# A decoder step on Trainium2: group norm, new rows, block compression and tables in one stage, with gates, down weights and route order moved

## The reference, cut to what matters

```python
mod = silu(c) @ w_ada + b_ada
h = rmsnorm(x) * (1 + sc1) + sh1
proj = h @ w_in
o_nsa, cmp_new, slc_new, win_state = nsa_group(proj, ...)
o_rwkv, wkv_T = rwkv_group(h, ...)
x = x + gt1 * (concat([o_nsa, o_rwkv]) @ w_out)
h2 = rmsnorm(x) * (1 + sc2) + sh2
eid, ew = hier_route(h2, ...)
x = x + gt2 * moe_ffn(h2, eid, ew, ...)
```

```python
y = (y - mean(y)) * rsqrt(var(y) + GN_EPS) * ln_x_w + ln_x_b
return (y + bonus) * g, S_T
```

## Time and profile before

| | |
|---|---|
| runs | 2575.92, 2577.76, 2578.44 us; median 2577.76 |
| the profiled execution | 2578.24 us, of which the trace spans 2576.1 |
| TensorE busy | 2268.1 us (88% of the span) |
| VectorE, ScalarE, GpSimd busy | 714.6, 358.2, 73.2 us |
| read from and written to HBM | 686.11 MB, 19.86 MB |

### The profile page before, as it was taken

How to read it: one execution, slowest core, us unless ns; L and a number is a source line. 1 busy time by engine, 2 the same in 40 slices (tenths; PEclk the granted TensorE clock), 3 DMA queues, 4 the chain that set the end, 5 groups by cost and what they waited for, 6 DMA issues and landing times. The chain is left out here.

```text
span 2576.1 us, 47327 instructions
## 1 busy us (share of the span) xinstructions
PE 2268.1 (88%) x20283; PEld 1619.4 (63%) x20283; DVE 714.6 (28%) x1979; ACT 358.2 (14%) x823; POOL 73.2 (3%) x122
## 2 busy tenths in 40 slices
PE   6899999799999968787766996999999999899997
PEld 4567667677777757664544774566656566566654
DVE  1111211340132145535655115111122111112224
ACT  1000110211210000013422003010011100000003
POOL 0000000000000000001011001000000000000000
PEclk9999999899999967776878997999999999999999
DMA  9887787533344430007669307999999999999993
GB/s 319 340 317 302 294 332 291 146 104 112 117 131 131 101 134 5 4 27 141 205 261 349 109 5 313 425 425 425 426 418 426 426 419 426 426 417 424 426 424 154
DMA packets 204971, 687.59 MB, mean 267 GB/s; under 512 B 38843, under 2 KB 84876, under 8 KB 165228
## 3 DMA queue, kind: packets, MB, share of 16 engines
q1 hardware_dynamic: 195746, 642.59, 64.1%
q0 software_dynamic: 6912, 38.28, 4.5%
q10 hardware_dynamic: 2180, 4.76, 0.5%
HBM read 686.11 MB, written 19.86 MB: 274 GB/s over the span
## 5 line engine op out<-in xcount | busy, mean ns | idle before, releaser
L2805 PE MATMUL bank<-sb_gate_w,sb_x_picked 128*64 128x256 f32 x2048 | 331.3, 389 | 49.7 <-DMA sb_up_w<-in_w_up_dram 49.7
L647 PE MATMUL bank<-sb_hT,sb_sample_kv 128*128 128x296 f32 (+1 forms) x1408 | 354.9, 412 | 12.3 <-PEq L494 12.3
L2805 PE MATMUL bank<-sb_up_w,sb_x_picked 128*64 128x256 f32 x2048 | 329.5, 387 | 0.0
L647 PEld LDWEIGHTS bank<-sb_hT,sb_sample_kv 128*128 128x128 f32 x1408 | 267.6, 191 | 94.4 <-issue 17.2
L2805 PEld LDWEIGHTS bank<-sb_gate_w,sb_x_picked 128*64 128x64 f32 x2048 | 175.0, 140 | 121.5 <-issue 77.4
L2829 PE MATMUL bank<-sb_down_w,sb_hiddenT 128*64 128x512 f32 x1024 | 226.8, 594 | 12.9 <-ACT sb_x_picked L2932 8.4
L469 PE MATMUL bank<-sb_cmp_xT,sb_cmp_w 128*128 128x254 f32 x1024 | 223.3, 379 | 6.6 <-ACT sb_cmp_xT L241 5.8
L469 PEld LDWEIGHTS bank<-sb_cmp_xT,sb_cmp_w 128*128 128x128 f32 x1024 | 193.2, 190 | 38.2 <-ACT sb_cmp_xT L241 7.3
L2805 PEld LDWEIGHTS bank<-sb_up_w,sb_x_picked 128*64 128x64 f32 x2048 | 178.3, 140 | 50.7 <-issue 3.6
L3051 DVE TENSOR_TENSOR sb_hidden<-sb_hidden,bank 128x256 f32<-128x256 f32 x32 | 13.5, 421 | 679.2 <-ACT sb_hidden L2940 679.2
L2829 PEld LDWEIGHTS bank<-sb_down_w,sb_hiddenT 128*64 128x64 f32 x1024 | 83.8, 137 | 133.2 <-issue 120.7
(11 more groups left out here) (576 smaller groups left out, 2280.7 us busy)
## 6 DMA issues: line engine op xcount, KB each, us to landing
sb_gate_w<-in_w_gate_dram SPq DMA_DIRECT2D x64, 2048.0 KB, 13.9
sb_up_w<-in_w_up_dram SPq DMA_DIRECT2D x64, 2048.0 KB, 18.3
sb_down_w<-in_w_down_dram SPq DMA_DIRECT2D x64, 2048.0 KB, 17.1
sb_w_ada<-in_w_ada_dram SPq DMA_DIRECT2D x48, 2048.0 KB, 11.1
sb_sample_kv<-in_w_in_dram SPq DMA_DIRECT2D x22, 2048.0 KB, 8.3
sb_sample_kv<-in_cache_cmp_kv_dram SPq DMA_DIRECT2D x128, 256.0 KB, 7.4
sb_sample_kv<-in_w_out_dram SPq DMA_DIRECT2D x16, 1024.0 KB, 11.4
sb_sample_kv<-in_state_win_kv_dram SPq DMA_DIRECT2D x8, 1024.0 KB, 16.9
```

The costliest lines, as they stand in the source:

```text
L647: ins = pe.matmul(bank[j % 4][:, 0:wide], ch[:, t, j % 2 * P:(j % 2 + 1) * P], hT[:, t, 0:wide], start=(t == 0), stop=(t == KT - 1))
L2805: ins = pe.matmul(bank[b][64 * half:64 * half + 64, col:col + 256], x[:, t, b * 64:b * 64 + 64], w[i][:, t % CK, half * 256:half * 256 + 256],
```

## The change

- `phase_groupnorm` and `phase_rows` become one block, `phase_groupnorm_rows`, without a barrier between. TensorE puts a quarter of the key compression behind each of the first four spreads and a group of transposes behind each of the last four; the value compression follows. All eight gated bonuses come before the reciprocal. VectorE keeps the eight products; the eight additions go to GpSimd. The sample tables are cut in two, with the second partial sum's copy between them. SP first waits for the scan's write of the prompt state.
- The eight gate writes and the two reads move from `write_rows` to SP's queue in the scan, ahead of the write of the prompt state; the combination of the sample branches waits for them.
- Of the first expert's loads, the two of the down weights move from the route to the expert block, behind a wait for the first gather.
- In the route TensorE transposes eight groups, computes the ranks, and then transposes the last four; ScalarE makes both exponentials before the seventh copy.
- Working buffers are placed in memory that the scan no longer needs (`k.home`); this changes addresses alone.

```diff
@@ phase_scan, SP
+                for b in range(NB):
+                    sp.dma_start(k.gate_dram[b].rearrange("h t j -> t j h"),
+                                 k.gates[TS * b:TS * (b + 1), 2, :].rearrange("t (j h) -> t j h", h=HEADS),
+                                 allow_slow_non_contiguous=True).then_inc(k.s_gate, 16)
+                sp.wait_ge(k.s_gate, 16 * NB)
+                for g in range(2):
+                    sp.dma_start(k.sgates[:, g, :], k.gate_dram[4 * g:4 * (g + 1)].rearrange("b h t j -> (b h t) j")).then_inc(k.s_gate, 16)
                 sp.wait_ge(s_oa, 2)
...
+def phase_groupnorm_rows(k, A):
...
+        @block.sync
+        def _(sp):
+            sp.wait_ge(k.s_state_out, 16)
...
+        @block.gpsimd
...
+            for spent in k.scan_spent:
+                pool.sem_clear(spent)
+            pool.wait_ge(s_a, RT)
+            for t in range(RT):
+                pool.wait_ge(s_w, t + 1)
+                pool.tensor_tensor(k.mixT[:, RT + t, :], k.bonus[:, t, :], k.y[:, t, :], ALU.add)
...
+        @block.tensor
...
+            def hidden(i, lo, hi):
+                if lo == 0:
                     pe.wait_ge(k.s_c_w[i], 16 * 2)
+                for s in range(lo, hi):
+                    j, at = s % 2, (CMP_T + 2 * i) * NT + s
+                    ins = pe.matmul(k.bank[7 - i][64 * j:64 * j + NC2, 0:P], chunks[:, at:at + CS * (NC2 - 1) + 1:CS],
+                                    w1[i][:, s, :], start=(s < 2), stop=(s >= CB - 2))
+                if hi == CB:
                     ins.then_inc(s_pre, 1)
...
+            pe.wait_ge(s_g, RT)
+            for m in range(2):
+                turned(m)
+            pe.wait_ge(s_e, 4)
+            pe.wait_ge(s_i, 1)
+            for t in range(RT):
+                if t >= 3:
+                    pe.wait_ge(s_w, t - 2)
+                pe.matmul(k.bank[(5, 0, 1)[t % 3]][:, 0:NT], spread[:, t, :], root, start=True, stop=True).then_inc(s_b, 1)
+                if t < 4:
+                    hidden(0, 8 * t, 8 * t + 8)
+                else:
+                    turned(t - 2)
+            hidden(1, 0, CB)
+            for m in range(6, 8):
+                turned(m)
+            pe.wait_ge(s_part, 2)
+            for i in range(2):
+                ins = pe.matmul(k.bank[7][:, 64 * i:64 * i + NC2], part[:, i, :], both, start=True, stop=True)
+            ins.then_inc(s_sum, 1)
+            turned(8)
+            pe.wait_ge(s_sil, 2)
+            compress_out(k, pe, NCP, w2, sil, s_out)
...
+        @block.vector
...
+            for t in range(RT):
+                dve.scalar_tensor_tensor(out=k.bonus[:, t, :], in0=k.bonus[:, t, :], scalar=k.par[:, C_LNB + t:C_LNB + t + 1],
+                                         in1=k.g[:, t, :], op0=ALU.add, op1=ALU.mult).then_inc(s_a, 1)
+            dve.wait_ge(s_r, 1)
+            dve.reciprocal(root, root).then_inc(s_i, 1)
...
+            for t in range(RT):
+                dve.wait_ge(s_b, t + 1)
+                dve.tensor_tensor(k.y[:, t, :], k.y[:, t, :], k.bank[(5, 0, 1)[t % 3]][:, 0:NT], ALU.mult).then_inc(s_w, 1)
+            part_copied(0)
+            dve.wait_ge(k.s_tab, 16)
+            dve.wait_ge(k.s_tm, 12)
+            row_tables(k, dve, step)
+            part_copied(1)
+            bias_tables(k, dve, step)
+            dve.wait_ge(s_out, 1)
...
@@ write_rows
-    for b in range(NB):
-        sp.dma_start(k.gate_dram[b].rearrange("h t j -> t j h"),
...
-    sp.wait_ge(s_gate, 16 * NB)
-    for g in range(2):
-        out(k.sgates[:, g, :], k.gate_dram[4 * g:4 * (g + 1)].rearrange("b h t j -> (b h t) j"))
     sp.wait_ge(s_o, 16 * n_out[0])
...
@@ phase_attend_samples, VectorE
+                    if s == 0:
+                        dve.wait_ge(k.s_gate, 16 * (NB + 2))
...
@@ phase_route, SP, TensorE, ScalarE
-                load_expert(k, A, sp, 0)
+                load_expert(k, A, sp, 0, parts=(0,))
...
-                for n in range(4 * NTT):
+                for n in range(8):
                     rows_turned(n)
                 pe.wait_ge(s_m, 1)
...
                 ins.then_inc(s_rank, 1)
+                for n in range(8, 4 * NTT):
+                    rows_turned(n)
...
-                for n in range(6, 9):
-                    rows_copied(n)
                 act.wait_ge(s_v2, 1)
                 act.activation(r1[:, :, 4:5], r1[:, :, 3:4], ACT.Exp).then_inc(s_e, 1)
-                for n in range(9, 4 * NTT):
+                for n in range(6, 4 * NTT):
                     rows_copied(n)
...
@@ phase_moe, SP
+                sp.wait_ge(s_gx, 16)
+                load_expert(k, A, sp, 0, parts=(1,))
                 load(0, 1, 1)
```

More of the change, by code:

```diff
@@ new lines, in phase_groupnorm_rows @@
+    own = k.dec[:, :, :].rearrange("p a n -> p (a n)")
+    sq, centre, gather = k.kk, own[:, 0:P], own[:, P:2 * P].rearrange("p (t h) -> p t h", t=RT)
+    spread, root = own[0:HT, 2 * P:2 * P + RT * P].rearrange("p (t n) -> p t n", t=RT), own[0:HT, 10 * P:10 * P + NT]
+    w1, w2, NC2 = k.c_w1, k.c_w2, NT // CS + NCP
+    work = k.a[:, :, :].rearrange("p a n -> p (a n)")
+    part, both = work[:, 0:2 * P].rearrange("p (i n) -> p i n", i=2), work[:, 2 * P:2 * P + NC2]
+    sil, far = work[:, 3 * P:3 * P + 4 * NCP].rearrange("p (i n) -> p i n", i=2), work[:, 4 * P:4 * P + TP]
@@ L1583, in write_rows @@
 def write_rows(k, A, sp, prefetch):
-    s_o, s_gate = k.sem("j_written"), k.sem("j_gates_written")
+    s_o = k.sem("j_written")
     n_out = [0]
@@ L1592, in write_rows @@
     r = lambda v: v.rearrange("s kv g d -> s (kv g d)")
-    for b in range(NB):
-        sp.dma_start(k.gate_dram[b].rearrange("h t j -> t j h"),
-                     k.gates[TS * b:TS * (b + 1), 2, :].rearrange("t (j h) -> t j h", h=HEADS),
-                     allow_slow_non_contiguous=True).then_inc(s_gate, 16)
     prefetch()
@@ L2631, in expert_buffers, with load_expert @@
     k.s_we = [k.sem(f"u_w_landed{i}") for i in range(6)]
-def load_expert(k, A, sp, e, free=None):
+def load_expert(k, A, sp, e, free=None, parts=(0, 1)):
     g_v, u_v = (v[0, bass.ds(e, 1)].rearrange("o (p k) n -> p (o k) n", p=P) for v in (A["w_gate"], A["w_up"]))
     d_v = A["w_down"][0, bass.ds(e, 1)].rearrange("o (k p) n -> p (o k) n", p=P)
-    for i in range(2):
+    for i in range(2) if 0 in parts else ():
         if free:
@@ L2642, in load_expert @@
         sp.dma_start(k.wu[i][:, :, :], u_v[:, i * CK:(i + 1) * CK, :]).then_inc(k.s_we[2 * i + 1], 16)
-    for i in range(2):
+    for i in range(2) if 1 in parts else ():
         if free:
@@ L3139, in step_kernel, with home @@
             k.c_w1 = [place[1].rearrange("p (s e) -> p s e", e=P), k.right("cmp_w_value", [P, CB, P], F32, cw)[:, :, :]]
-            phase_groupnorm(k, A)
-            rw.close()
-            with ExitStack() as own:
-                k.kcTp, k.vcp = k.sb("kcT_prompt", [P, 2 * NCP], F32, own), k.sb("vc_prompt", [NCP, KVW], F32, own)
-                k.kvrows = k.sb("kvrows", [P, len(ROWS), 3 * ROW], F32, own)
+            spent, taken = k.rkvT[:, :, :].rearrange("p a n -> p (a n)"), [0]
+            def home(n):
+                taken[0] += n
+                return spent[:, taken[0] - n:taken[0]]
+            k.home = home
+            with kept:
+                k.kcTp, k.vcp = home(2 * NCP), home(KVW)
+                k.kvrows = home(len(ROWS) * 3 * ROW).rearrange("p (i n) -> p i n", i=len(ROWS))
                 k.zero_rows = k.pT[:, SLC_T + 2:SLC_T + 4, :].rearrange("p a n -> p (a n)")[:, 0:ROW]
-                phase_rows(k, A, own)
+                phase_groupnorm_rows(k, A)
+                rw.close()
                 cw.close()
```

327 lines of the change are left out of this document (132 added, 195 removed).

## The result

The changed kernel takes 2560.70 us (median of six executions, 2556.13 to 2565.60) against 2577.75 us before (six, 2574.05 to 2578.76): ratio 0.9938, 95% interval 0.9927 to 0.9950, 17.05 us less. The profiled execution took 2562.45 us with a span of 2560.5, so 15.8 less than the profiled one of before. Forecast were 2555.4 and 22.3 less. The time lies inside the stated range of 2548 to 2566, and 0.7 above 2550 to 2560, the forecast's own. The sum hides more than it shows: one term of it all but vanished, and others came out better.

The account below looks back on a forecast made before the run. Bound: a row of barriered stages ahead of the expert stage, whose weight loads have fixed length. Terms -11.1 - 7.8 - 5.4 + 0.5 + 1.5 = -22.3 gave a median of 2555.4 us; own range 2550 to 2560, stated range 2548 to 2566.

Parts of the forecast that it names:

- Part 1: Group norm and rows merged into one stage: the next stage starts 12.7 to 9.4 us earlier, taken as 11.1.
- the eight steps: Merged stage: eight spreads on TensorE, alternating with key-compression quarters, then transposes, take 9.6 to 12.8 us at full clock.
- Rival B: TensorE falls to its low clock in the merged stage: gain 1 instead of 11.1, time 2565.5; chance 0.09.
- The tail: Merged stage: behind the last product, VectorE's copies and tables take 9.2 us and end the stage.
- Part 2: Eight group-norm additions moved to GpSimd: +0.5 us for holding VectorE up, bounds 0 and 3.6.
- Rival C: GpSimd's additions block VectorE in the merged stage: 3.6 instead of 0.5, as much again in the tables, 2562; chance 0.05.
- Part 3: Gates moved to the scan: compute ends the prompt attention, 7.8 us gained, bounds 3 and 8.5; scan price +1.5.
- rival A: SP still ends the prompt attention: gain 3 instead of 7.8, time 2560.2; chance 0.09.
- the 1.5: Scan: price in us of the gate writes moved there, bounds 0 and 6.0.
- Rival E: Gate writes starve TensorE's instruction supply in the scan: +54 in place of +1.5, time 2608; chance 0.03.
- Part 4: Down weights moved, route reordered: first gather starts near 1575 instead of 1580.6, gain 5.4 us, bounds 3 and 6.
- Rival D: Down weights push back the second expert's loads by 10 us, time 2565; chance 0.05.

Follow-up runs that it names:

- run 5: Changed kernel with four extra products, results unused, in TensorE's pause ahead of the first spread: ratio 0.9862 to before, median 2544.84 us.
- run 3: Changed kernel with the four groups of transposes moved ahead of the wait for the reciprocal, into TensorE's pause: ratio 0.9876 to before.
- run 10: Changed kernel with the four groups of transposes moved into TensorE's pause and the eight additions back on VectorE: ratio 0.9894 to before.
- run 6: Changed kernel with the gate writes and reads back in the prompt attention: ratio 0.9950 to before.
- run 1: The changed kernel measured again with no edit: ratio 0.9929 to before, median 2558.17 us.
- run 4: Changed kernel with the whole key compression ahead of the first spread, then eight spreads back to back and the transposes: ratio 0.9903 to before.
- run 11: Changed kernel with transposes in TensorE's pause, row tables before the first product, bias tables cut in two, an early small Silu: ratio 0.9863, median 2541.72 us.

## Why the prediction was right, point by point

**Sign and range: right**, with the sum 5.3 too hopeful for the median. That is partly luck: the largest term, half of the sum, came to 1.45 instead of 11.1, and the time stayed in the range because that range also held the rivals, and because three other terms came out 3.5 better than forecast. What the terms did:

- **Part 1, the merged stage: wrong.** The step that failed is "the eight steps take 9.6 to 12.8 us". They took 1184.81 - 1164.78 = 20.0, because TensorE ran at the lower clock. With the clock up (run 5) they take 1180.13 - 1168.08 = 12.05, inside what was forecast, and the next stage starts 21.84 behind the reciprocal, where the forecast meant 19.5 to 22.8. So the working was right for a clock that the kernel did not get. Rival B had the mechanism, and a gain of 1 where 1.45 was measured, but only 0.09, on the ground that "there is no pause now for it to fall in". That ground was at odds with the working itself: the products still wait for the reciprocal. The pause of before was 2.65, the two groups of transposes put into it take 1.09 (0.94 by the working's own 0.47 a group), so some 1.6 was left to be read off. That rival B's gain comes so close is luck too: it had 18.3 for the steps, which took 20.0, and 7.4 for the value compression, which took 4.82 because the clock came back inside it; as a whole it gave 2565.5.
- **The tail: right in size, wrong in owner.** VectorE was forecast to end the stage with 9.2. In the changed kernel it waits 1.40 for the value compression, slowed to 4.82, and the stage ends 11.0 behind the last product. With the clock up (run 3) it is VectorE, in 10.0, of which 0.6 is the copies stretched by GpSimd.
- **Part 2, the additions: 0** instead of +0.5. They take 0.79 each, within the bound of 1.45, and in the changed kernel no product waits for one. Rival C fell for the products. The Trainium skill, page SBUF — State Buffer, section Who interferes with whom, bears on both halves of run 10. It says that a VectorE instruction with at most one SBUF input, outside the modes that use two ports, does not contend with GpSimd; the products at 0.46 agree. It also says that copies can enter such a mode and then do contend; the 1.40 against 0.76 agrees, though no run shows in which mode the copies ran. The prediction had left that condition out.
- **Part 3, the gates: right, 8.9 against 7.8**, a little over the bound of 8.5. Compute ends the attention; SP's last issue ends 29 us ahead of ScalarE's last write, so rival A fell. The scan as a whole shows no price (251.40 against 251.64), but its ninth rows copy came 2.6 later than before, with 3.7 lost where the gate writes run, and what follows that copy was 2.8 shorter, for a reason that no run shows. So the 1.5 is left open by run 6. Rival E, +54, fell.
- **Part 4: right, 6.1 against 5.4.** The third write landed at 1559.64 + 2.8 = 1562.4, ahead of the index. Rival D fell: the first down product follows the gather by 25.03, before by 25.41. In other executions the route took 2.6 to 2.8 more (run 1: 33.60), so 5.4 is as good a figure as 6.1. What the forecast left out is that the index itself comes about 1 earlier (29.93 behind the route's first load instead of 30.94).

By terms: 9.15 lost in the merged stage, 1.7 + 1.1 + 0.7 won back in scan, attention and route; the samples, the experts and what lies ahead, for which nothing was forecast, differ by 1.0 in sum.

## What to carry to other kernels

Where work is moved in between dependent steps to fill an engine, work out what is left of each wait after the move: here 1.6 us of an unfilled pause ahead of light steps cost 9 us behind it. Filling it, even with products that nobody reads (run 5), gave that back, and putting dense work right behind it kept the clock up too (run 4). A rival that has its price from a row of this very kernel (the clock of 0.50 in the same place before) deserves more than a sentence against it. When a stage misses its forecast, compare the length of one repeated step with the granted clock beside it before blaming the engines that were given new work.

## What the runs showed of the hardware that was not expected

- A TensorE that the records call busy without a break kept the lower clock for 20 us (1167 to 1187) in the changed kernel, while the same four mixed steps, entered without a pause, kept the higher one (runs 3, 5, 10 and 11, all four). A pause of 2.28 ahead of the dense key compression left the clock at 1.00 (run 4).
- GpSimd's additions stretch some VectorE instructions that read SBUF alone: four copies of 32x32 took 1.40 instead of 0.76, and 2.44 in run 4, where more of the additions lay beside them; in run 11 the first bias table took 0.43 and the second 0.86, where run 5 has 0.24 and 0.31.
- Element-wise writes can hold their queue for long, and by very different lengths: the eight gate writes took SP 5.32 in the scan of the changed kernel, 13.50 in the attention of before and 30.12 in run 6. GpSimd's page gathers ran beside both of the last two; what makes the difference stays open.
- Stages that no edit touched differ between executions: samples and output 277.1 to 281.2, the route at one and the same order 30.7 to 33.6. About 24 us into the route the granted clock was 1.00 in the first profile and 0.50 in run 1, the longest; why stays open.
